# Moving the two buffers of split weights to the far end of SBUF

## The chip, the cores and the metric

The kernel runs on one core of one Trainium2 chip. The metric is the device time of one execution in microseconds (us), less is better.

## What the reference computes

A stack of transformer-like blocks in float32 on 512 positions of width 1024. Almost all its arithmetic is in dense projections, of which only the shapes matter here; what is computed between them is shown by name.

```python
# first block: norm, input projection 1024 -> 4096, two branches, output projection 2048 -> 1024
u = rms_norm(h, norm_in_g[l])
proj = jnp.einsum('bsd,de->bse', u, w_in[l])
pool_x, pool_z, m_x, m_z = jnp.split(proj, ...)
y_pool = pool_mixer(pool_x, ...) * jax.nn.silu(pool_z)
y_m = mlstm_branch(m_x, ...) * jax.nn.silu(m_z)
h = h + jnp.einsum('bse,ed->bsd', jnp.concatenate([y_pool, y_m], -1), w_out[l])
# second block, two layers: attention (nsa, then swa), then a feed-forward with a short convolution
x = x + mixer(rms_norm_2(x, norm_mix[i]), ...)
a, u = jnp.split(h @ w_gu, 2, axis=-1)          # 1024 -> 2 x 2816
x = x + (jax.nn.silu(causal_depthwise_conv(a, ...)) * u) @ w_down   # 2816 -> 1024
```

## The kernel before

All activations live in SBUF as eight channel tiles of 128 partitions x 512 positions. Every dense projection is made of **weight tiles**: one is 1024 x 128 weights, stored in SBUF as [128, 8, 128] float32 (4 KB in each partition). There are 227 of them, always in one fixed order, in these stages: "in" 32 tiles, "wo_pool" and "wo_m" 8 each, "nsa" 21, "nsa_o" 8, "gu0" 44, "down0" 22, "swa" 10, "swa_o" 8, "gu1" 44, "down1" 22.

To keep float32 accuracy at the rate of the `float32r` type, both operands are split into a high and a low part, and each product is made of three matmuls: high x high, high weights x low activations, low weights x high activations. So a weight tile costs 8 x 3 = 24 matmuls of 128 x 128 weights on 512 columns, 5448 in all. They are written at three places of the code with the same body: L1304 to L1306 (`channel_major`), L1602 to L1604 (the loop of the "gu" stages), L1616 to L1618 (the "down" stages).

Four engines work in a chain on the weight tiles, tied by semaphores alone:

- SyncE (SP) loads tile w into `raw`, which has 4 slots, by one transfer of 512 KB, once POOL has split tile w-4.
- GpSimd (POOL) waits until the matmuls of tile w-2 are done (`tile_used`), then makes the high part, L334: `WH[w % 2] = raw + 0`, and from it the low part, L337: `WL[w % 2] = raw - WH[w % 2]`. `WH` and `WL` have 2 slots each. They are the buffers that the change moves.
- TensorE (PE) waits for the split (`tile_split`) and for a free PSUM bank (`freed`) and does the 24 matmuls. Its weights come from `WH` and `WL`, its moving operand from `XH` and `XL`, the split activations.
- VectorE (DVE) and ScalarE (ACT) take the results out of PSUM, do all the elementwise work on buffers in `arena`, and write `XH` and `XL`.

Everything that isn't named by itself (intermediate tensors of each stage, of the attentions too) is carved out of one buffer, `arena`, of 30712 float32 per partition. Matmuls outside of the projections read both operands from it, as L1342 (32 records of 128 x 512, plain float32) does.

SBUF buffers are placed one behind the other in the order of their declaration. In KB from the first one, per partition:

| buffer | before | after |
|---|---|---|
| `resid` | 0 to 16 | same |
| `x_hi` (`XH`) | 16 to 32 | same |
| `x_lo` (`XL`) | 32 to 48 | same |
| `raw` | 48 to 64 | same |
| `w_hi` (`WH`) | 64 to 72 | 199.4 to 207.4 |
| `w_lo` (`WL`) | 72 to 80 | 191.4 to 199.4 |
| nine small ones (`cols`, `ident`, `masks`, `rstd`, ...) | 80 to 87.4 | 64 to 71.4 |
| `arena` | 87.4 to 207.4 | 71.4 to 191.4 |
| `zero`, `mv`, `rv`, `dn` | from 207.4 | same |

These lines declare them (`P` is 128, `KT` 8, `S` 512, `RAW` 4, `SPL` 2):

```python
R = sb("resid", [P, KT, S])
XH = sb("x_hi", [P, KT, S], F32R)
XL = sb("x_lo", [P, KT, S], F32R)
raw = sb("raw", [P, RAW, KT, P])
WH = sb("w_hi", [P, SPL, KT, P], F32R)
WL = sb("w_lo", [P, SPL, KT, P], F32R)
```

and these lines read the moved buffers, in `channel_major`:

```python
mm(out, WH[:, s, k], XH[:, k], start=(k == 0), stop=False)
mm(out, WH[:, s, k], XL[:, k], start=False, stop=False)
ins = mm(out, WL[:, s, k], XH[:, k], start=False, stop=(k == KT - 1))
```

Of the kernel before, what the change touches and what calls it, by code (L numbers as in the profile page):

```python
# [18 lines left out]
F32R = mybir.dt.float32r  # L19
# [5 lines left out]
P = 128  # L25
# [3 lines left out]
KT = D // P  # L29
# [22 lines left out]
SPL = 2  # L52
# [65 lines left out]
def build(nc, a):  # L118
    with ExitStack() as ctx:
        def sb(name, shape, dt=F32):  # L120
            return ctx.enter_context(nc.sbuf_tensor("sb_" + name, shape, dt))
# [6 lines left out]
        XH = sb("x_hi", [P, KT, S], F32R)  # L128
        XL = sb("x_lo", [P, KT, S], F32R)
        raw = sb("raw", [P, RAW, KT, P])  # L130
        WH = sb("w_hi", [P, SPL, KT, P], F32R)
        WL = sb("w_lo", [P, SPL, KT, P], F32R)
        cols = sb("cols", [P, NCOL])
        rows = sb("rows", [P, NROW])
        ident = sb("ident", [P, P])
# [6 lines left out]
        PS = ctx.enter_context(nc.psum_tensor("ps", [P, 8, S], F32))  # L142
        NA = 30712
        arena = sb("arena", [P, NA])

        def col(name, k=0):
            return cols[:, COLS[name] + k:COLS[name] + k + 1]
# [146 lines left out]
        def psum(bank, n=S):  # L294
            return PS[:, bank, 0:n]
# [32 lines left out]
        def _(pool):  # L328
            def split(it, s, first=False):

                pool.wait_ge(raw_in[s], 16 * (it + 1))
                if not first:
                    pool.wait_ge(tile_used, 4 * it + (s - SPL + 1))
                nc.gpsimd.tensor_tensor(WH[:, s % SPL], raw[:, s], zero.unsqueeze(2).broadcast_to([P, KT, P]), ALU.add  # L334
                                        ).then_inc(hi_made, 1)
                pool.wait_ge(hi_made, 4 * it + (s + 1))
                nc.gpsimd.tensor_tensor(WL[:, s % SPL], raw[:, s], WH[:, s % SPL].bitcast(F32),  # L337
                                        ALU.subtract).then_inc(tile_split, 1)
# [933 lines left out]
        def _(pe):  # L1272
# [19 lines left out]
            def channel_major(stage, j, n, xname=None):  # L1292
# [6 lines left out]
                for k in range(KT):  # L1299
# [3 lines left out]
                    out = psum(t % 2)  # L1303
# [3 lines that stand above are left out]
                ins.then_inc(tile_used, 1)  # L1307
# [280 lines left out]
            def ffn(layer, q):  # L1588
# [7 lines left out]
                with pe.Fori(1, FT // 2) as it:  # L1596
                    for b in range(4):
# [3 lines left out]
                        for k in range(KT):  # L1601
# [3 lines that stand above are left out]
                        ins.then_inc(tile_used, 1)  # L1605
                pe.wait_ge(freed, t0 + 2 * FT - 1)
                last = (t0 + 2 * FT - 1) % 2
                for f in range(FT):
# [4 lines left out]
                    for k in (sorted(range(KT), key=lambda k: k == last) if f == 0 else range(KT)):  # L1613
# [3 lines left out]
                        mm(psum(k), WH[:, s, k], XL[:, x], start=False, stop=False)  # L1617
                        ins = mm(psum(k), WL[:, s, k], XH[:, x], start=False, stop=(f == FT - 1))  # L1618
                        if f == FT - 1 and k < KT - 1:
# [151 lines left out]
```

## Time and profile before

| | |
|---|---|
| median of 2 runs | 1889.88 us (1889.49 to 1890.26) |
| span of the profiled execution | 1889.5 us |
| instructions | 22388 |
| PE busy | 1708.0 us, 90% of the span |
| DVE busy | 1169.6 us, 62% |
| POOL busy | 1058.6 us, 56% |
| mean granted TensorE clock | 0.961 |

The span reaches from the first to the last instruction; the timed executions stand within 0.8 us of it. Records of matmuls overlap, since the engine is pipelined: what tells its pace is the time from one start to the next, not the length of a record.

### The profile page before, as it was taken

To read this page: it belongs to the slowest core of one execution; us is meant where nothing else is said; L and a number is where in the kernel's file an instruction comes from. 1 tells how busy PE (TensorE), PEld (TensorE's weight loads), DVE (VectorE), ACT (ScalarE), POOL (GpSimd) and SP (SyncE) were. 2 spreads that over 40 slices of the span, in tenths; PEclk is the share of its full clock that TensorE was granted. 3 is DMA by queue.
4 is the path that set the end of the run, shared out by engine and by line. 5 is a ranking of instruction groups with operands and counts; after the bars stand their busy time and mean duration, and the time that the engine had idled before them with its cause. 6 is when DMAs were issued, how large, how long until landed. Compare 5 with 4: busy or idle time off the path is not lost.

```text
span 1889.5 us, 22388 instructions
## 1 busy us (share of the span) xinstructions
PE 1708.0 (90%) x8180; PEld 1346.3 (71%) x8180; DVE 1169.6 (62%) x1503; ACT 386.3 (20%) x719; POOL 1058.6 (56%) x472
## 2 busy tenths in 40 slices
PE   6688999898877979999899998998799899998996
PEld 4566845566666867778688887886678788887885
DVE  7995133557898347764676776336954576767334
ACT  3000123332200134442211111112143211111112
POOL 5566712137665310003688887886701688888784
PEclk8899999999988989999999999999989999999998
DMA  5122301014221100001233332332200223333231
GB/s 212 57 88 67 101 23 34 12 45 150 78 78 56 45 23 1 1 1 34 78 100 89 100 100 78 99 91 89 89 1 12 84 94 90 99 100 90 80 98 56
DMA packets 37545, 133.47 MB, mean 71 GB/s; under 512 B 4560, under 2 KB 4960, under 8 KB 36960
## 3 DMA queue, kind: packets, MB, share of 16 engines
q1 hardware_dynamic: 34992, 123.22, 21.3%
q10 hardware_dynamic: 2480, 9.22, 1.3%
q8 instruction: 52, 0.85, 0.2%
q14 instruction: 21, 0.17, 0.0%
HBM read 130.33 MB, written 2.10 MB: 70 GB/s over the span
## 4 chain that ended last, share of the span: by engine, by line
PE 75%; DVE 19%; issue 2%; ACT 2%; POOL 1%; DMA 0%; DVEq 0%; ACTq 0%; SPq 0%; POOLq 0%
PE ps L1602 8%; PE ps L1603 8%; PE ps L1604 8%; PE ps L1304 7%; PE ps L1305 7%; PE ps L1306 7%; PE ps L1563 5%; PE ps L1616 4%; PE ps L1618 4%; PE ps L1617 4%; PE ps L1531 3%; PE ps L1546 2%; DVE sb_arena L764 2%; DVE sb_arena L992 2%; PE ps L1331 2%
## 5 line engine op out<-in xcount | busy, mean ns | idle before, releaser
L334 POOL TENSOR_TENSOR sb_w_hi<-sb_raw,sb_zero 128x1024 fp32r<-128x1024 f32 x227 | 449.7, 1981 | 778.5 <-PE ps L1306 663.8
L337 POOL TENSOR_TENSOR sb_w_lo<-sb_raw,sb_w_hi 128x1024 fp32r<-128x1024 f32 x227 | 590.7, 2602 | 17.8
L1304 PE MATMUL ps<-sb_x_hi,sb_w_hi 128*128 128x512 f32 x824 | 340.8, 414 | 97.3 <-DVE sb_arena L971 24.6
L1305 PE MATMUL ps<-sb_x_lo,sb_w_hi 128*128 128x512 f32 x824 | 330.9, 402 | 0.0
L1306 PE MATMUL ps<-sb_x_hi,sb_w_lo 128*128 128x512 f32 x824 | 330.1, 401 | 0.0
L1304 PEld LDWEIGHTS ps<-sb_x_hi,sb_w_hi 128*128 128x128 f32 x824 | 161.6, 196 | 150.0 <-issue 28.9
L1602 PE MATMUL ps<-sb_x_hi,sb_w_hi 128*128 128x512 f32 x640 | 249.8, 390 | 0.0
L1604 PE MATMUL ps<-sb_x_hi,sb_w_lo 128*128 128x512 f32 x640 | 249.3, 389 | 0.0
L1603 PE MATMUL ps<-sb_x_lo,sb_w_hi 128*128 128x512 f32 x640 | 249.2, 389 | 0.0
L1306 PEld LDWEIGHTS ps<-sb_x_hi,sb_w_lo 128*128 128x128 f32 x824 | 160.8, 195 | 35.6
L1305 PEld LDWEIGHTS ps<-sb_x_lo,sb_w_hi 128*128 128x128 f32 x824 | 161.6, 196 | 33.7 <-issue 1.7
L1189 DVE TENSOR_TENSOR sb_x_lo<-sb_arena,sb_x_hi 128x512 fp32r<-128x512 f32 x44 | 77.2, 1765 | 134.5 <-ACT sb_x_hi L625 134.5
L1616 PE MATMUL ps<-sb_x_hi,sb_w_hi 128*128 128x512 f32 x352 | 139.0, 395 | 11.5 <-DVE sb_x_lo L1189 11.5
L1602 PEld LDWEIGHTS ps<-sb_x_hi,sb_w_hi 128*128 128x128 f32 x640 | 120.1, 188 | 29.6 <-POOL sb_w_lo L337 3.3
L1617 PE MATMUL ps<-sb_x_lo,sb_w_hi 128*128 128x512 f32 x352 | 138.6, 394 | 0.0
L1618 PE MATMUL ps<-sb_x_hi,sb_w_lo 128*128 128x512 f32 x352 | 138.4, 393 | 0.0
L1604 PEld LDWEIGHTS ps<-sb_x_hi,sb_w_lo 128*128 128x128 f32 x640 | 120.1, 188 | 25.4
L1603 PEld LDWEIGHTS ps<-sb_x_lo,sb_w_hi 128*128 128x128 f32 x640 | 120.2, 188 | 23.6
L1201 DVE SCALAR_TENSOR_TENSOR sb_arena<-sb_arena,sb_cols 128x512 f32<-128x512 f32 x44 | 112.4, 2554 | 6.7 <-DVE sb_arena L1199 6.7
L617 ACT ACTIVATE sb_arena<-sb_arena 128x512 f32<-128x512 f32 x44 | 27.8, 633 | 416.6 <-DVE sb_arena L1203 416.6
L1563 PE MATMUL ps<-sb_arena 128*128 128x96 f32 x864 | 105.4, 274 | 0.0
L1563 PEld LDWEIGHTS ps<-sb_arena 128*128 128x128 f32 x864 | 101.9, 193 | 0.0
(240 smaller groups left out, 2182.3 us busy)
## 6 DMA issues: line engine op xcount, KB each, us to landing
sb_raw<-in_w SPq DMA_DIRECT2D x227, 512.0 KB, 3.6
sb_resid<-in_x SPq DMA_DIRECT2D x8, 256.0 KB, 5.5
sb_arena<-in_cmp_w1k ACTq DMA_DIRECT2D x1, 2048.0 KB, 11.0
sb_arena<-in_cmp_w1v ACTq DMA_DIRECT2D x1, 2048.0 KB, 14.2
out<-sb_resid SPq DMA_DIRECT2D x8, 256.0 KB, 2.1
sb_arena<-in_pool_w ACTq DMA_DIRECT2D x1, 1024.0 KB, 5.0
sb_arena<-in_invc ACTq DMA_DIRECT2D x1, 1024.0 KB, 7.0
sb_arena<-in_wg ACTq DMA_DIRECT2D x1, 768.0 KB, 8.4
```

Source lines behind the costliest of these rows:

```text
L334: nc.gpsimd.tensor_tensor(WH[:, s % SPL], raw[:, s], zero.unsqueeze(2).broadcast_to([P, KT, P]), ALU.add).then_inc(hi_made, 1)
L337: nc.gpsimd.tensor_tensor(WL[:, s % SPL], raw[:, s], WH[:, s % SPL].bitcast(F32), ALU.subtract).then_inc(tile_split, 1)
L1304: mm(out, WH[:, s, k], XH[:, k], start=(k == 0), stop=False)
L1305: mm(out, WH[:, s, k], XL[:, k], start=False, stop=False)
L1306: ins = mm(out, WL[:, s, k], XH[:, k], start=False, stop=(k == KT - 1))
L1563: ins = mm(PS[:, v % 2, to:to + VN], PT_[:, v % 2, hh, p0:p0 + P], v_rows[0 if swa else m][:, at:at + VN], start=(n == 0), stop=(n == len( ...
L1602: mm(out, WH[:, s, k], XH[:, k], start=(k == 0), stop=False)
L1603: mm(out, WH[:, s, k], XL[:, k], start=False, stop=False)
L1604: ins = mm(out, WL[:, s, k], XH[:, k], start=False, stop=(k == KT - 1))
L1616: mm(psum(k), WH[:, s, k], XH[:, x], start=(f == 0), stop=False)
L1617: mm(psum(k), WH[:, s, k], XL[:, x], start=False, stop=False)
L1618: ins = mm(psum(k), WL[:, s, k], XH[:, x], start=False, stop=(f == FT - 1))
```

## The change

`WH` and `WL` are declared behind `arena` instead of behind `raw`, in the order `WL`, `WH`. Everything that stood between (the small buffers and `arena`) moves down by 16 KB. The sizes, the number of slots and every instruction of every engine, with its order and its waits, are the same; only SBUF addresses differ. All shifts of `WH`, `WL` and `arena` are multiples of 128 bytes.

```diff
         raw = sb("raw", [P, RAW, KT, P])
-        WH = sb("w_hi", [P, SPL, KT, P], F32R)
-        WL = sb("w_lo", [P, SPL, KT, P], F32R)
         cols = sb("cols", [P, NCOL])
         rows = sb("rows", [P, NROW])
...
         NA = 30712
         arena = sb("arena", [P, NA])
+        WL = sb("w_lo", [P, SPL, KT, P], F32R)
+        WH = sb("w_hi", [P, SPL, KT, P], F32R)
```

## Rows read from the trace of the kernel before

**Rows 1.** The page: busy time, and tenths busy in 40 slices

```profile
PE 1708.0 (90%) x8180; PEld 1346.3 (71%) x8180; DVE 1169.6 (62%) x1503; ACT 386.3 (20%) x719; POOL 1058.6 (56%) x472
...
PEclk8899999999988989999999999999989999999998
```

**Rows 2.** Busy time of each engine in the stages gu0, down0 and nsa_o

```profile
core 0: us, PE busy (x) PEld busy (x) DVE busy (x) ACT busy (x) POOL busy (x), PEclk, DMA share, GB/s
...
870.00:913.50 43.50, 43.50 (x195) 35.92 (x192) 16.95 (x17) 5.70 (x10) 31.66 (x14) 1.00 0.25 73
919.30:1163.80 244.50, 243.63 (x1058) 198.62 (x1058) 170.14 (x139) 29.63 (x36) 198.70 (x86) 0.99 0.31 92
1169.80:1290.90 121.10, 121.03 (x528) 100.08 (x528) 40.06 (x28) 11.18 (x18) 95.95 (x42) 0.99 0.32 96
```

**Rows 3.** Groups: line, engine, operation, count | busy us, mean ns | idle before

```profile
L337 POOL TENSOR_TENSOR sb_w_lo<-sb_raw,sb_w_hi 128x1024 fp32r<-128x1024 f32 x227 | 590.7, 2602 | 17.8
L334 POOL TENSOR_TENSOR sb_w_hi<-sb_raw,sb_zero 128x1024 fp32r<-128x1024 f32 x227 | 449.7, 1981 | 778.5 <-PE ps L1306 663.8 <-PE ps L1604 59.5 <-PE ps L1618 48.4
L1304 PE MATMUL ps<-sb_x_hi,sb_w_hi 128*128 128x512 f32 x824 | 340.8, 414 | 97.3 <-DVE sb_arena L971 24.6 <-DVE sb_x_lo L683 23.7 <-DVE sb_arena L779 14.9
L1602 PE MATMUL ps<-sb_x_hi,sb_w_hi 128*128 128x512 f32 x640 | 249.8, 390 | 0.0
L1616 PE MATMUL ps<-sb_x_hi,sb_w_hi 128*128 128x512 f32 x352 | 139.0, 395 | 11.5 <-DVE sb_x_lo L1189 11.5
```

**Rows 4.** PE in gu0: first matmuls of two tiles, 24 apart

```profile
1011.10 0.39 PE L1602 MATMUL ps<-sb_x_hi,sb_w_hi 128*128 128x512 f32 x1
...
1016.54 0.40 PE L1602 MATMUL ps<-sb_x_hi,sb_w_hi 128*128 128x512 f32 x1
```

**Rows 5.** PE in nsa_o while POOL is idle, three matmuls apart, and POOL's next instruction

```profile
872.83 0.39 PE L1304 MATMUL ps<-sb_x_hi,sb_w_hi 128*128 128x512 f32 x1
...
873.51 0.39 PE L1304 MATMUL ps<-sb_x_hi,sb_w_hi 128*128 128x512 f32 x1
...
875.86 1.90 POOL L334 TENSOR_TENSOR sb_w_hi<-sb_raw,sb_zero 128x1024 fp32r<-128x1024 f32 x1 [194.94 <-PE ps L1306]
```

**Rows 6.** PE in order of time: arena operands at full clock; projections at half clock

```profile
12.80 0.63 PE L1304 MATMUL ps<-sb_x_hi,sb_w_hi 128*128 128x512 f32 x1
13.23 0.63 PE L1305 MATMUL ps<-sb_x_lo,sb_w_hi 128*128 128x512 f32 x1
...
238.81 13.90 PE L1342 MATMUL ps<-sb_arena 128*128 128x512 f32 x32
```

**Rows 7.** Line L1342 by itself: duration of one record, ns, least, median, most

```profile
L1342 PE MATMUL ps<-sb_arena x32: 590/592/595, 238.8 to 252.1; 128*128 128x512 f32 x32
```

**Rows 8.** POOL over two tiles of gu0, and the weight load that waits for it

```profile
1005.94 1.90 POOL L334 TENSOR_TENSOR sb_w_hi<-sb_raw,sb_zero 128x1024 fp32r<-128x1024 f32 x1 [0.50 <-PE ps L1604]
1007.92 2.46 POOL L337 TENSOR_TENSOR sb_w_lo<-sb_raw,sb_w_hi 128x1024 fp32r<-128x1024 f32 x1
1011.41 2.17 POOL L334 TENSOR_TENSOR sb_w_hi<-sb_raw,sb_zero 128x1024 fp32r<-128x1024 f32 x1 [1.04 <-PE ps L1604]
1013.66 2.72 POOL L337 TENSOR_TENSOR sb_w_lo<-sb_raw,sb_w_hi 128x1024 fp32r<-128x1024 f32 x1
1016.43 0.19 PEld L1602 LDWEIGHTS ps<-sb_x_hi,sb_w_hi 128*128 128x128 f32 x1 [0.16 <-POOL sb_w_lo L337]
```

**Rows 9.** Line L337 by itself: durations, and who waited for it

```profile
L337 POOL TENSOR_TENSOR sb_w_lo<-sb_raw,sb_w_hi x227: 2339/2717/3247, 7.1 to 1861.1; 128x1024 fp32r<-128x1024 f32 x114
...
  PEld ps L1602: 3.3, 19
```

**Rows 10.** Line L358, POOL on two inputs in the arena

```profile
L358 POOL TENSOR_TENSOR sb_arena<-sb_arena x8: 1265/1722/1735, 428.6 to 441.4; 128x512 f32<-128x512 f32 x8
```

**Rows 11.** POOL in down0, one tile

```profile
1253.28 1.90 POOL L334 TENSOR_TENSOR sb_w_hi<-sb_raw,sb_zero 128x1024 fp32r<-128x1024 f32 x1 [0.81 <-PE ps L1618]
1255.26 2.72 POOL L337 TENSOR_TENSOR sb_w_lo<-sb_raw,sb_w_hi 128x1024 fp32r<-128x1024 f32 x1
```

## Prediction, made before the change was run

> **What bounds the kernel now.** I read the page first. TensorE is busy for 90% of the span, and its granted clock is at nine tenths or more in nearly all slices [rows 1]. So the question is what sets the pace of PE, and where it waits. The view of the stages answers both: in gu0, down0 and nsa_o PE is busy for all but 1 us or less of the whole stretch [rows 2]. These stages, with gu1, down1 and swa_o, which have the same code, are 148 of the 227 weight tiles (44 + 22 + 44 + 22 + 8 + 8), and there the end moves only if a tile of 24 matmuls takes another time, or if PE has to wait for its weights.
>
> The pace: the same matmul of two neighbouring tiles of gu0 starts at 1011.10 and at 1016.54, 24 matmuls apart, which is 5.44 us or **226.7 ns** for each [rows 4]. There are 3 x (824 + 640 + 352) = 5448 such matmuls [rows 3], and 5448 x 226.7 ns = 1235 us, 65% of the span. This is the number that a placement of buffers could touch with the greatest effect.
>
> The weights: POOL makes them just in time. In gu0 it sits idle for 0.50 us before one tile and 1.04 us before the next, always until PE frees the slot; the split of the second takes 2.17 + 2.72 us against 1.90 + 2.46, since DVE works in the arena beside it; and at its end PE's weight load waits for it, by 0.16 us [rows 8]. Over the run these waits of L1602 come to 3.3 us in 19 places [rows 9]. So one tile in two of the gu stages has about 0.03 us of slack (0.50 less the handover of some 0.47 that the waiting tile leaves), the other about 0.54; in down0 POOL idles 0.81 us [rows 11], a slack of 0.31.
>
> **The change part by part.** No instruction is added, removed or moved on any engine, so there is no term for issue, for waits or for DMAs. Three things have another address: the targets of POOL's L334 and L337, the weights that PE loads for the 5448 matmuls, and everything in the arena, 16 KB lower. Each is costed by asking whether the trace shows any time that depends on where an operand lies, or on two engines being in the same region.
>
> 1. *PE reading weights while others write beside them.* If POOL's writes into `WH` and `WL`, or transfers into `raw` next to them, disturbed PE, its pace would differ when POOL is idle. POOL is idle for 194.94 us before its L334 at 875.86; in that time the matmuls of L1304 at 872.83 and 873.51 are three apart, 0.68 us, or 226.7 ns each, as in gu0 under a busy POOL [rows 5, 4]. POOL's traffic costs PE nothing, so moving it away gives nothing: 0 us.
>
> 2. *PE's two own reads, weights and moving operand, colliding.* The tile of rows 4 covers eight k slices of `WH`, of `WL`, of `XH` and of `XL`, at distances from some 16 to some 64 KB from each other, and its neighbour the other slot. If 226.7 ns depended on those distances, single starts would differ. They do not: 23 intervals of a tile that starts without a wait are 0.22 or 0.23 us. The pace in nsa_o is that of gu0 though both slots are used there. I take 0 us. What speaks for a gain is that 226.7 is not the best the engine shows. At half clock the same matmuls start 0.43 us apart, that is 512 columns at 1.2 GHz and nothing on top [rows 6], so 213.3 would be the counterpart at 2.4 GHz. And the 32 records of L1342, whose operands both lie in the arena, span 13.90 us with a last record of 0.59, so 13.31 / 31 = 429.4 ns for twice the work of a split matmul, 214.7 for its share [rows 6, 7]. The difference of 12.0 ns on each of 5448 is 65 us at most; but L1342 is plain float32 at half the column rate, so the type explains the difference at least as well as the place. The bounds are 0 and -65 us, and I take the end 0, since it goes by rows of the same instruction.
>
> The Trainium skill, page TensorE: Matmul & The Clock Gate, section "Wait — 56ns, not 53.3ns?", gives a spacing of N / 2.4 GHz plus about 2.5 ns, 215.7 ns for 512 columns, for a stream at full clock. This trace disagrees for split matmuls, with 226.7 [rows 4]. By the page's figure each would have 11 ns to lose, an estimate of 60 us for all; the same page gives weight loads and moving operands read ports of their own (section "Step-by-step: what each phase is for"), which leaves no collision that a move could undo.
>
> 3. *POOL's two passes.* They write to a new place. POOL's other elementwise work shows what another place costs: L358 works on 512 elements with both inputs and the output in the arena, 30 KB and more from `WH`, and takes 1265 ns at the least; L337 takes 2339 at the least for 1024 [rows 10, 9]. The second 512 elements cost 1074 ns, 2.1 ns an element, and leave 191 ns for the start of an instruction, so one rate with one start-up fits both places. So 0 us. As a bound I allow 5% either way of the 4.58 us of a split (2602 + 1981 ns, rows 3), 0.23 us, because eight records of L358 can't show less. Dearer, it would cost 0.23 - 0.03 = 0.20 us on 44 tiles of the gu stages, 8.8 us, and nothing where the slack is 0.31 or more. Cheaper, it would save the waits of 3.3 us, and I allow 1.7 us for slower first matmuls behind them: -5 us.
>
> 4. *Arena and small buffers 16 KB lower.* DVE, ACT and PE read and write them at hundreds of different offsets already, and the shift is a multiple of 128 bytes, so no pattern inside a line changes. 0 us; bound included in that of point 3, since DVE matters to the end mainly through POOL.
>
> The sum is 0: the profiled execution would again have a span of 1889.5 us, and the median, which was 0.4 us above that, 1889.9. The forecast is **1889.9 us**, with bounds of its own of -5 and +8.8, so 1885 to 1898.7.
>
> **The rivals.** *Faster: weights and activations stop colliding.* The one state in which PE does 512 columns in less time is L1342, and the move makes the distance between `WH`/`WL` and `XH`/`XL` large, some 150 KB and more instead of 16 to 64. If the 12 ns per matmul were a matter of sharing a region, a tile would take 24 x 214.7 = 5.15 us, 0.29 less. But not all of that is granted: in the gu stages every second tile is then limited by POOL and gains 0.03 only, so 44 x 0.29 + 44 x 0.03 = 14.1 us; down0 and down1, 44 x 0.29 = 12.8 (slack 0.31); nsa_o, swa_o, wo_pool and wo_m, 32 x 0.29 = 9.3; in, nsa and swa, 63 tiles, where PE waits for DVE often (L1304 has 97.3 us of idle time before it [rows 3]), between 0 and 18.3, say 9. Sum 45 us: **1845 us** (1836 to 1854). Against it: the pace is uniform over all distances in a tile, and the excess is gone at half clock. Chance 0.09.
>
> *Slower: POOL becomes the bound.* If POOL writes or reads back more slowly near the end of SBUF, every split grows by some d. It decides from d = 0.03 us on, in every second tile of gu0 and gu1, where PE already waits for L337 [rows 8, 9]. The price is 44 x (d - 0.03) + 60 x (d - 0.31), the second term for down0, down1, nsa_o and swa_o. 2% or 37.8 us is reached at d = 0.56 us, a split dearer by 12%. With 15%, 0.69 us, it is 29 + 23 + 44 x 0.15 for the other gu tiles = 58 us: **1948 us**. For it speaks only that POOL has so little slack; against it the one rate of point 3. Chance 0.04.
>
> *It isn't a change at all.* That buffers are declared in another order and land where they did is excluded by the sizes, which put `w_lo` at 191.4 KB. That the move matters to nothing is the forecast itself.
>
> **How the numbers follow.** Forecast 0.87, faster rival 0.09, slower rival 0.04. The range needs 8 in 10; the forecast's own case with its bounds gives that, so it stays with 1884 to 1898 (its +8.8 rounded down, its -5 widened by 1 us for clock windows that fall otherwise; 2 of the executions shown differ by 0.8). A change of 2%, 37.8 us, is about what a measurement of this kernel can tell from none. The faster rival's 1836 to 1854 lies on both sides of 1852, mostly under it, so faster by over 2% gets 0.07. Slower by over 2% gets 0.03, as a POOL dearer by 5 to 12% stays within it. Within 2%: 0.90.
>
> **What would show it in the profile after.** Starts of L1602, L1304 and L1616 still 0.22 or 0.23 us apart (5.44 us a tile): points 1 and 2 hold. Starts 0.215 apart: the faster rival. L334 at 1.90 us without DVE beside it and L337 at 2.34 to 2.72, POOL idle 0.5 and 1.0 us in turn in gu0: point 3 holds. L337 beyond 2.9, and waits of PE's weight loads for L337 well over 3.3 us in total: the slower rival. DVE's groups within 1% of before: point 4. The prediction is wrong if an engine's time depends on the region of SBUF in a way that this layout, with `WH` and `WL` always between `raw` and the small buffers, gave no chance to see; the uniform pace only speaks for distances under 64 KB.

## The result and the profile after

The changed kernel takes 1916.12 us (1915.7 to 1916.55, 2 runs) against 1889.88: ratio 1.0138, 95% interval [1.0119, 1.0157]. That is 26.2 us slower, outside the forecast range of 1884 to 1898. The profiled execution has a span of 1913.9 us, 24.4 more than before, at the same mean granted clock, 0.961.

First the groups of the kernel after, as [rows 3] (count | busy us, mean ns | idle before):

```profile
L337 POOL TENSOR_TENSOR sb_w_lo<-sb_raw,sb_w_hi 128x1024 fp32r<-128x1024 f32 x227 | 592.8, 2611 | 17.8
L334 POOL TENSOR_TENSOR sb_w_hi<-sb_raw,sb_zero 128x1024 fp32r<-128x1024 f32 x227 | 445.4, 1962 | 804.8 <-PE ps L1306 671.1 <-PE ps L1604 73.1 <-PE ps L1618 53.7
L1304 PE MATMUL ps<-sb_x_hi,sb_w_hi 128*128 128x512 f32 x824 | 344.4, 418 | 91.9 <-DVE sb_x_lo L683 30.2 <-DVE sb_arena L971 24.0 <-DVE sb_arena L779 11.7
...
L1602 PE MATMUL ps<-sb_x_hi,sb_w_hi 128*128 128x512 f32 x640 | 252.7, 395 | 0.0
```

POOL, the engine of the slower rival, is not slower: L337 went from 2602 to 2611 ns in the mean, L334 from 1981 to 1962, and POOL waits longer for PE than before (804.8 us against 778.5). It is the matmuls that take longer. The line of L1602 by itself, as the source view shows it, has no wait for POOL left, where [rows 9] had 3.3 us in 19 places:

```profile
L1602 PEld LDWEIGHTS ps<-sb_x_hi,sb_w_hi x640: 187/188/192, 946.9 to 1762.2; 128*128 128x128 f32 x160
L1602 PE MATMUL ps<-sb_x_hi,sb_w_hi x640: 390/393/404, 947.1 to 1762.5; 128*128 128x512 f32 x160
its engine sat idle before it (us, times) until:
who waited for it (us, times):
```

The pace is read from starts, as in [rows 4]. PE in gu1 after, first matmuls of two tiles, 24 apart, and a piece of the stream from the first of them:

```profile
1572.75 0.40 PE L1602 MATMUL ps<-sb_x_hi,sb_w_hi 128*128 128x512 f32 x1
1572.98 0.39 PE L1603 MATMUL ps<-sb_x_lo,sb_w_hi 128*128 128x512 f32 x1
1573.21 0.40 PE L1604 MATMUL ps<-sb_x_hi,sb_w_lo 128*128 128x512 f32 x1
1573.45 0.39 PE L1602 MATMUL ps<-sb_x_hi,sb_w_hi 128*128 128x512 f32 x1
...
1578.35 0.40 PE L1602 MATMUL ps<-sb_x_hi,sb_w_hi 128*128 128x512 f32 x1
```

A tile takes 5.60 us here, 233.3 ns a matmul, where it took 5.44 and 226.7. The nanoseconds of the trace show the difference more plainly than two decimals. Before, the starts of an undisturbed tile are 227, 226, 227, 227, 226, 227 ns apart and so on, and in the stages at full clock a tile that began late falls back into that within eleven matmuls at most. After, they never settle on one interval: in gu1 they alternate 238, 229, 238, 229 (mean 233.3), and in gu0 and the down stages they repeat 230, 233, 241, 232, 231, 232, 228, seven in a round with a mean of 232.4. The round of seven drifts through tiles of 24, so it belongs neither to a k slice nor to a slot. POOL has no part in it: it rests for 194.7 us before its L334 at 876.84, and in that time the 23 matmuls of nsa_o from 871.19 to 876.53 take 5.34 us, 232.2 ns each, where the kernel before had 226.7 [rows 5].

At half clock nothing changed, and neither did L1342, plain float32 from the arena. The second tells little: both of its operands lie in the arena, so the change left their distance as it was. After, PE at 11.44 us, and line L1342 by itself, to be held against [rows 6, 7]:

```profile
11.44 0.63 PE L1304 MATMUL ps<-sb_x_hi,sb_w_hi 128*128 128x512 f32 x1
11.86 0.63 PE L1305 MATMUL ps<-sb_x_lo,sb_w_hi 128*128 128x512 f32 x1
```

```profile
L1342 PE MATMUL ps<-sb_arena x32: 590/592/592, 237.4 to 250.7; 128*128 128x512 f32 x32
```

Where the 24.4 us lie is seen in the windows from the first to the last matmul of each stage. After, for nsa_o, gu0 and down0, then swa, gu1 and down1 (columns as in [rows 2]):

```profile
870.80:915.40 44.60, 44.60 (x195) 36.14 (x193) 17.04 (x17) 5.79 (x10) 31.72 (x14) 1.00 0.23 71
921.10:1170.10 249.00, 248.06 (x1058) 200.15 (x1058) 170.46 (x139) 29.77 (x36) 197.04 (x86) 0.99 0.29 91
1176.00:1300.60 124.60, 124.55 (x528) 100.81 (x528) 40.18 (x28) 11.17 (x18) 96.18 (x42) 0.98 0.30 93
1303.40:1374.10 70.70, 62.12 (x242) 47.86 (x242) 64.30 (x61) 15.22 (x24) 44.83 (x19) 0.91 0.22 68
...
1512.40:1763.00 250.60, 250.00 (x1058) 200.35 (x1058) 168.91 (x139) 29.71 (x36) 197.69 (x86) 0.99 0.29 90
1768.80:1893.90 125.10, 124.96 (x528) 101.21 (x529) 40.28 (x28) 14.62 (x24) 91.83 (x40) 0.98 0.23 72
```

The same windows of the kernel before, for swa, gu1 and down1:

```profile
1293.80:1360.40 66.60, 59.77 (x242) 46.84 (x242) 62.26 (x60) 15.15 (x24) 44.81 (x19) 0.95 0.25 72
...
1497.40:1741.00 243.60, 242.75 (x1058) 198.26 (x1058) 168.51 (x139) 29.71 (x36) 199.24 (x86) 0.99 0.31 93
1747.00:1869.60 122.60, 122.53 (x528) 101.23 (x529) 40.19 (x28) 14.68 (x24) 91.64 (x40) 0.98 0.24 73
```

Against these and [rows 2], gu0 grew by 4.5 us (244.5 to 249.0), down0 by 3.5, nsa_o by 1.1, swa by 4.1, gu1 by 7.0, down1 by 2.5. The same windows give 2.4 for nsa (186.5 to 188.9), 1.2 for swa_o (43.5 to 44.7), 0 for the two "wo" stages together and -1.4 for "in". Full price would be 24 x 5.8 ns = 0.14 us for a tile at a pace of 232.5, or 6.1 us for 44 tiles, and 0.16 us or 7.0 us at the 233.3 of gu1. From the start of the fifth tile to that of the last the two stages pay less, 4.7 us instead of 5.4 in gu0 and 5.5 instead of 6.2 in gu1: their former waits for POOL and the slow first matmuls behind them went away.

Most of the rest is clock. In the first 6 us of gu1 the granted clock was 0.74 before and 0.52 after, and the first tile took 1.3 us more; in gu0 it was 0.63 and 0.74, and the first tile took 0.6 us less. Part of what swa lost is clock too: 0.95 before, 0.91 after. In "in" the last tiles, which follow one another without a wait, did grow by 0.16 us each; the stage as a whole, where PE waits for DVE and for transfers and the stretches of half clock fell otherwise, did not.

### The profile page after: what moved, and what is told of

Same layout as the page of the kernel before. It is cut to its first block, busy times and chain, and to the rows that moved or that the text cites. A ratio compares the mean times of both kernels' runs of the same rounds, so it can differ in the third digit from the quotient of the medians.

```text
span 1913.9 us, 22388 instructions
## 1 busy us (share of the span) xinstructions
PE 1737.9 (91%) x8180; PEld 1354.7 (71%) x8180; DVE 1171.4 (61%) x1503; ACT 386.2 (20%) x719; POOL 1056.4 (55%) x472
## 4 chain that ended last, share of the span: by engine, by line
PE 75%; DVE 19%; issue 2%; ACT 2%; POOL 1%; DMA 0%; DVEq 0%; ACTq 0%; SPq 0%; POOLq 0%
PE ps L1603 8%; PE ps L1602 8%; PE ps L1604 8%; PE ps L1304 7%; PE ps L1305 7%; PE ps L1306 7%; PE ps L1563 5%; PE ps L1616 4%; PE ps L1617 4%; PE ps L1618 4%; PE ps L1531 3%; PE ps L1546 2%; DVE sb_arena L764 2%; DVE sb_arena L992 2%; PE ps L1331 1%
## 5 line engine op out<-in xcount | busy, mean ns | idle before, releaser
L334 POOL TENSOR_TENSOR sb_w_hi<-sb_raw,sb_zero 128x1024 fp32r<-128x1024 f32 x227 | 445.4, 1962 | 804.8 <-PE ps L1306 671.1
L337 POOL TENSOR_TENSOR sb_w_lo<-sb_raw,sb_w_hi 128x1024 fp32r<-128x1024 f32 x227 | 592.8, 2611 | 17.8
L1304 PE MATMUL ps<-sb_x_hi,sb_w_hi 128*128 128x512 f32 x824 | 344.4, 418 | 91.9 <-DVE sb_x_lo L683 30.2
L1305 PE MATMUL ps<-sb_x_lo,sb_w_hi 128*128 128x512 f32 x824 | 335.9, 408 | 0.0
L1306 PE MATMUL ps<-sb_x_hi,sb_w_lo 128*128 128x512 f32 x824 | 335.6, 407 | 0.0
L1604 PE MATMUL ps<-sb_x_hi,sb_w_lo 128*128 128x512 f32 x640 | 252.7, 395 | 0.0
L1602 PE MATMUL ps<-sb_x_hi,sb_w_hi 128*128 128x512 f32 x640 | 252.7, 395 | 0.0
L1603 PE MATMUL ps<-sb_x_lo,sb_w_hi 128*128 128x512 f32 x640 | 252.6, 395 | 0.0
L1616 PE MATMUL ps<-sb_x_hi,sb_w_hi 128*128 128x512 f32 x352 | 140.9, 400 | 11.3 <-DVE sb_x_lo L1189 11.3
L1602 PEld LDWEIGHTS ps<-sb_x_hi,sb_w_hi 128*128 128x128 f32 x640 | 120.3, 188 | 28.8
L1604 PEld LDWEIGHTS ps<-sb_x_hi,sb_w_lo 128*128 128x128 f32 x640 | 120.3, 188 | 28.6
L1617 PE MATMUL ps<-sb_x_lo,sb_w_hi 128*128 128x512 f32 x352 | 140.5, 399 | 0.0
L1618 PE MATMUL ps<-sb_x_hi,sb_w_lo 128*128 128x512 f32 x352 | 140.4, 399 | 0.0
L1201 DVE SCALAR_TENSOR_TENSOR sb_arena<-sb_arena,sb_cols 128x512 f32<-128x512 f32 x44 | 112.7, 2560 | 6.7 <-DVE sb_arena L1199 6.7
```

The lines of the kernel that those rows point to most:

```text
L1616: mm(psum(k), WH[:, s, k], XH[:, x], start=(f == 0), stop=False)
```

## The experiments

All addresses that matter are put in one number here, the **phase**: the address of a weight buffer less that of the activations, modulo 256 bytes. Within `WH`, `WL`, `XH`, `XL` a k slice is 512 or 2048 bytes and a slot 4096, so all slices of a buffer have one phase. The kernel before has phase 0, since its buffers of 16 and 8 KB follow each other without a gap. The changed one has 128: the small buffers and the arena that now lie ahead add up to 384 bytes more than a multiple of 512, and 384 is 128 more than 256.

The first theory, formed on the trace above: the pace depends on the phase, not on how far the buffers are apart. The rival: it depends on the region, since the weights lie far from the activations or near the end of SBUF. A third: the shift of the arena did it. A fourth is left open by the first runs: the weights moved by 128 bytes against `raw` too, from which POOL makes them, and not only against the activations.

### Far away, old phase

`WH`, `WL` behind arena and `ident`; the arena is 120 words shorter, which no stage uses; the rest of the small buffers last.

```diff
+NA = 30592
 R = sb("resid", [P, KT, S])
...
 raw = sb("raw", [P, RAW, KT, P])
+arena = sb("arena", [P, NA])
+ident = sb("ident", [P, P])
 WH = sb("w_hi", [P, SPL, KT, P], F32R)
 WL = sb("w_lo", [P, SPL, KT, P], F32R)
```

> The two buffers lie behind the arena (120 KB and more above the activations) as in the changed kernel, but at addresses that are the old ones modulo 4096 bytes, so modulo 512 the weights and the activations stand to each other as before. Theory of the phase (the pace of split matmuls depends on where weights and moving operand lie to each other within some 512 bytes): 226.7 ns from start to start as before, time within 0.3% of 1889.9 us. Rival, the region (far from the activations, or high in SBUF, weights are read more slowly): 232 to 233 ns, 1914 to 1918 us.

Measured: 1890.08 us (10 runs), ratio 1.0 [0.999, 1.001]. The pace is 226.7 ns in every stage; first matmuls of two neighbouring tiles of down0:

```profile
1209.61 0.39 PE L1616 MATMUL ps<-sb_x_hi,sb_w_hi 128*128 128x512 f32 x1
...
1215.05 0.39 PE L1616 MATMUL ps<-sb_x_hi,sb_w_hi 128*128 128x512 f32 x1
```

5.44 us, as before. The region rival is dead, and so is an effect of the arena's shift, which here is 23.4 KB instead of 16.

### Near, new phase

Four small buffers (taken from their old places) lie between `raw` and the weights.

```diff
 raw = sb("raw", [P, RAW, KT, P])
-WH = sb("w_hi", [P, SPL, KT, P], F32R)
-WL = sb("w_lo", [P, SPL, KT, P], F32R)
+rstd = sb("rstd", [P, S])
+cmask = sb("cmask", [P, NT, P], BF16)
+rows = sb("rows", [P, NROW])
+mv = sb("mv", [P, 16, 2])
+WL = sb("w_lo", [P, SPL, KT, P], F32R)
+WH = sb("w_hi", [P, SPL, KT, P], F32R)
```

> The two buffers stay next to the activations, 3.4 KB above their old place, at addresses that are those of the changed kernel modulo 4096 (rstd, cmask, rows and mv lie between raw and them; the arena hardly moves). Theory of the phase: the slow pace, 232 to 233 ns a matmul, 1912 to 1920 us. Rival, the region: 226.7 ns, 1890 us. A third theory, that the arena's shift by 16 KB did it: 226.7 ns, 1890 us as well.

Measured: 1916.04 us (4 runs), ratio 1.0144 [1.0127, 1.0161], the whole loss of the change with the two buffers 3.4 KB above their old place. Tiles of down0:

```profile
1218.80 0.40 PE L1616 MATMUL ps<-sb_x_hi,sb_w_hi 128*128 128x512 f32 x1
...
1224.37 0.39 PE L1616 MATMUL ps<-sb_x_hi,sb_w_hi 128*128 128x512 f32 x1
```

5.57 us a tile, 232.1 ns, and the same round of seven intervals in the trace as in the changed kernel.

### Everything 128 bytes up

```diff
+sb("gap0", [P, 32])
 R = sb("resid", [P, KT, S])
```

> Every buffer lies 128 bytes higher, in the old order, so all distances stay and all absolute addresses modulo 512 change. If only the distance between weights and moving operand counts: 226.7 ns, 1890 us. If the absolute address of the weights modulo 256 or 512 counts (before 128, in the changed kernel 0, here 256): another pace than 226.7, about that of the changed kernel or worse, over 1905 us. The region rival expects 1890 us.

Measured: 1890.18 us (10 runs), ratio 1.0001 [0.9992, 1.0011], pace 226.7 ns. The distance counts, not the address.

### Two phases in one kernel

The two slots become buffers of their own; slot 0 gets phase 128, slot 1 256, which is 0 again.

```diff
+sb("gap0", [P, 32])
+WH0 = sb("w_hi0", [P, KT, P], F32R)
+WL0 = sb("w_lo0", [P, KT, P], F32R)
+sb("gap1", [P, 32])
+WH1 = sb("w_hi1", [P, KT, P], F32R)
+WL1 = sb("w_lo1", [P, KT, P], F32R)
```

> Slot 0 of both weight buffers lies 128 bytes further from the activations than before (modulo 512), slot 1 256 bytes further; both near. Tiles alternate between the slots, so the trace shows a pace for each. Theory of the phase: at least one of the two slots shows another pace than 226.7 ns, as the changed kernel does at 384 bytes; if the period is 256 bytes, slot 1 shows 226.7 and slot 0 what the changed kernel shows, 232 to 233. The region rival: 226.7 in both.

Measured: 1905.18 us in one run, somewhat over half of the loss. Tiles alternate. First matmuls of three tiles of down0 (L1631 is L1616 of the kernel before):

```profile
1213.67 0.40 PE L1631 MATMUL ps<-sb_x_hi,sb_w_hi 128*128 128x512 f32 x1
...
1219.26 0.39 PE L1631 MATMUL ps<-sb_x_hi,sb_w_hi 128*128 128x512 f32 x1
...
1224.71 0.40 PE L1631 MATMUL ps<-sb_x_hi,sb_w_hi 128*128 128x512 f32 x1
```

Slot 0 takes 5.59 us, slot 1 5.45. So the period is 256 bytes: with a divisor of it, slot 0 would be fast too. It also takes the last doubt from the run before: slot 0 of `WH` lies at the very address that `WH` had there, and is slow here, since the activations are 128 bytes lower.

### The other phases

The same two-slot form with other gaps: 64 and 128 bytes for the first run, 32 and 64 for the second, 160 (slot 1 first) and 64 for the third; for the fourth the high and low part of a slot are one buffer that is read from its fifth word on.

> Both weight slots near; slot 0 stands 64 bytes, slot 1 192 bytes further from the activations than before. 0 and 256 gave 226.7 ns, 128 and 384 gave 232.5. If what counts is one address bit of weight 128 (two halves of 128 bytes each in a period of 256), the value at 64 should be that of 0 or of 128, and one of 64 and 192 like 226.7 and the other like 232.5, or both between. If the pace grows evenly with the distance from a multiple of 256, both slots show about 229.6. A pace under 226.7 at 64 or 192 would make a faster kernel than both, by some 5 us for each ns.

> As the run at 64 and 192, with slot 0 at 32 bytes and slot 1 at 96 bytes. An address bit of weight 128 that is compared at the start of the buffers would leave 226.7 in both; an even growth gives about 228.2 and 231.1; with finer structure, anything else. No figure is forecast beyond the span from 215 to 240 ns.

> Near, slot 0 at 224 and slot 1 at 160 bytes modulo 256. With 0 at 226.7 ns, 32 at 233.5, 64 at 233.3, 96 at 234.5, 128 at 232.5 and 192 at 228.7, a smooth course would give 227 to 229 at 224 and 229 to 232 at 160. A value under 226.7 would show that the old place isn't the best; else 0 stays the only good one.

> Near, slot 0 at 16 and slot 1 at 240 bytes modulo 256 (high and low part of a slot in one buffer). If the chip works on lines of 32 bytes, 16 is as 0 or as 32 (226.7 or 233.5), and 240 as 224; if the course is smooth, 240 is within 1 ns of 226.7. It tells how exact the placement has to be.

Measured: 1915.47, 1915.44, 1920.09 and 1912.21 us, one run each. The pace by phase is the median over the tiles of gu0 at full clock, from a tile's eleventh matmul on, out of the starts in the traces. It takes in only 13 intervals of a tile, so a round that does not fit into them moves it: over whole tiles phase 16 has 233.0, phase 96 has 234.0, phase 160 has 233.0.

| phase, bytes | ns a matmul in gu0 | elsewhere |
|---|---|---|
| 0 | 226.7 | same |
| 16 | 233.4 | 226.7 in down0 |
| 32 | 233.5 | same |
| 64 | 233.5 | 233.2 in down0 |
| 96 | 234.5 | same |
| 128 | 232.5 | 233.3 (whole tiles) in gu1 of the changed kernel |
| 160 | 233.6 | same |
| 192 | 228.8 and 233.4, tile by tile | the same two in gu1, 228.7 in down0 |
| 224 | 233.3 | same |
| 240 | 228.4 | 226.6 in down0 |

None of my guesses of a form held: no single address bit, no even growth, no smooth course. Phase 0 is the only one that has 226.7 throughout; most others give 232 to 234.5, and 16 and 240 fall back to 226.7 in one stage. None is below 226.7 but for rounding.

Phase 192 has two paces in one stage. Its tiles in slot 1 alternate between them in gu0 and in gu1, though PE reads the same addresses in each. First matmuls of one such tile and the next tile, then of the following one in slot 1 (L1617 is L1602 of the kernel before):

```profile
994.07 0.40 PE L1617 MATMUL ps<-sb_x_hi,sb_w_hi 128*128 128x512 f32 x1
...
999.58 0.40 PE L1617 MATMUL ps<-sb_x_hi,sb_w_hi 128*128 128x512 f32 x1
...
1005.17 0.40 PE L1617 MATMUL ps<-sb_x_hi,sb_w_hi 128*128 128x512 f32 x1
...
1010.78 0.39 PE L1617 MATMUL ps<-sb_x_hi,sb_w_hi 128*128 128x512 f32 x1
```

The one takes 5.51 us, the other 5.61. So at this phase the pace depends on something beside PE's addresses, the state in which the stream comes into a tile, say; no run shows what. With two phases in one kernel, the value of one slot may also owe something to its neighbour.

### Which operand

First the parts of the weights apart: slot 0 has `WH` at 128 and `WL` at 0, slot 1 the reverse.

```diff
+WH1 = sb("w_hi1", [P, KT, P], F32R)
+WL0 = sb("w_lo0", [P, KT, P], F32R)
+sb("gap0", [P, 32])
+WH0 = sb("w_hi0", [P, KT, P], F32R)
+WL1 = sb("w_lo1", [P, KT, P], F32R)
```

> Slot 0 has its high part at 128 bytes and its low part at 0, slot 1 the high part at 0 and the low part at 128. If each of the 24 matmuls is slowed by the weight load that runs beside it, at 128 alone, the slot with two of three loads at 128 (slot 0) gets about 230.6 ns in the mean and the other about 228.6; if one pair alone is responsible, one slot shows 226.7 and the other 232.5.

Measured: 1917.38 us in one run; slot 0 233.2 ns, slot 1 231.2. Slot 1, with its low part alone at 128, repeats three intervals in the trace: 226 from the high-high matmul to the next, then 234 and 233 or 234. A piece of gu0 (L1616 to L1618 are L1602 to L1604 of the kernel before):

```profile
1016.09 0.39 PE L1616 MATMUL ps<-sb_x_hi,sb_w_hi 128*128 128x512 f32 x1
1016.31 0.40 PE L1617 MATMUL ps<-sb_x_lo,sb_w_hi 128*128 128x512 f32 x1
1016.54 0.40 PE L1618 MATMUL ps<-sb_x_hi,sb_w_lo 128*128 128x512 f32 x1
1016.78 0.39 PE L1616 MATMUL ps<-sb_x_hi,sb_w_hi 128*128 128x512 f32 x1
```

The load of the low weights starts in the trace with the matmul that streams `XL`, at 1016.32. That matmul's step to the next is slow (234 ns), and so is the step after it; the record of the load itself stays at 0.19 us. So one bad load in three costs more than a third, 4.5 ns of the 5.8, and two in three (slot 0) cost more than all three: 6.5 ns. The means of 228.6 and 230.6 that I expected for single prices that add up are refuted.

Then the activations: `XL` goes 128 bytes up, `raw` and the weights 256, so the weights have phase 0 to `XH` and to `raw` and 128 to `XL` alone.

```diff
 XH = sb("x_hi", [P, KT, S], F32R)
+sb("gap0", [P, 32])
 XL = sb("x_lo", [P, KT, S], F32R)
+sb("gap1", [P, 32])
 raw = sb("raw", [P, RAW, KT, P])
```

> The weights stay at 0 to the high activations, and the low activations are moved by 128 bytes against both, so one matmul in three streams an operand that stands at 128 to the weights. If only the distance between the weights being loaded and the operand being streamed counts: a mean between 226.7 and 232.5, some 228.6 ns. If the distance of weights to high activations alone counts: 226.7.

Measured: 1913.85 us in one run; 230.8 ns in gu0 and nsa_o, 233.3 in gu1 and both down stages. The weights kept their phase to `XH`, so the streamed operand is the partner in it. They kept it to `raw` too, which answers the fourth rival: what this run has in common with all slow ones is that weights and `XL` stand to each other at another phase than 0. The size was again above the proportional guess.

### The change with its phase mended

```diff
-        NA = 30712
+        NA = 30616
         arena = sb("arena", [P, NA])
         WL = sb("w_lo", [P, SPL, KT, P], F32R)
         WH = sb("w_hi", [P, SPL, KT, P], F32R)
```

> The changed kernel with an arena that is 96 words (384 bytes) shorter, words that no stage uses: the two buffers lie at 191 KB as in the change, and at a multiple of 256 bytes from the activations. If the distance modulo 256 is all that made the change slower: 226.7 ns a matmul and 1889 to 1891 us. If something else of this layout costs too (the order of the two buffers, the arena's place), it stays above 1895 us.

Measured: 1890.91 us (11 runs), ratio to the kernel before 1.0002 [0.9993, 1.0011]. 384 bytes less of unused arena take back the whole loss. Its groups read as those of before:

```profile
L337 POOL TENSOR_TENSOR sb_w_lo<-sb_raw,sb_w_hi 128x1024 fp32r<-128x1024 f32 x227 | 590.0, 2599 | 17.8
L334 POOL TENSOR_TENSOR sb_w_hi<-sb_raw,sb_zero 128x1024 fp32r<-128x1024 f32 x227 | 449.3, 1979 | 779.2 <-PE ps L1306 664.1 <-PE ps L1604 59.3 <-PE ps L1618 48.5
L1304 PE MATMUL ps<-sb_x_hi,sb_w_hi 128*128 128x512 f32 x824 | 341.8, 415 | 94.6 <-DVE sb_arena L971 24.6 <-DVE sb_x_lo L683 24.1 <-DVE sb_arena L759 14.4
```

No version beats the kernel before; with phase 0 the place is free to choose.

## Why the prediction was wrong, point by point

The reading of the bound was right: PE's pace is what sets the end, and the loss is a matter of that pace alone. I had named it as the number that a placement could touch with the greatest effect, and then costed it at 0.

**Point 2 failed**, "PE's two own reads, weights and moving operand, colliding", taken at the end 0 with bounds of 0 and -65 us. The whole loss belongs to it, +26.2 us in the time and +24.4 in the span: the run with the phase mended takes it back. It is 5448 matmuls at up to 5.8 or 6.6 ns each, less what waits and clock gave back. The argument was that a tile covers many distances, from 16 to 64 KB, and shows one pace. But all those distances are multiples of 512 bytes, so the two tiles sample one phase 48 times. It could speak for the region, where it was right (the run far away shows 0 us), and not for the low bits of the address. My closing caveat went the same wrong way: it doubted distances beyond 64 KB, not the phase. The bound had the wrong side as well: I asked what would be gained if a collision stopped, not what would be lost if the old layout was the good one of its kind. The exact pace of 226.7 [rows 4, 5] is what one phase gives as well as what no dependence gives; I took it as proof of the second.

**Point 4** rested on the same slip: "a multiple of 128 bytes, so no pattern inside a line changes". The period is 256 bytes, and the weights moved by 128 against it. For the arena itself the point held: DVE's L1201 took 2554 ns before and 2560 after, and L1342 kept its 592 ns.

**Point 1** held: far from or near to POOL's and the transfers' targets, the pace is that of the phase. **Point 3** held: L334 and L337 kept their durations within 1% at a place 119 and 135 KB further up, and the slower rival's mechanism did not occur (POOL's idle time grew).

**The faster rival** had the right pair of operands and the wrong variable and sign. Its 12 ns over L1342 are not phase: no phase among ten came below 226.7. The slower side had a chance of 0.04 for POOL alone; a slower PE was not among the cases. That the time stayed within 2%, to which the prediction gave 0.90, came true for another reason than the one given.

The Trainium skill, page SBUF — State Buffer, section "Who interferes with whom", says that PE and ACT never wait on anyone, and the page TensorE: Matmul & The Clock Gate, section "Step-by-step: what each phase is for", gives weight loads and moving operand read ports of their own. By the two together the ten phases would be equal. The measurements decide against that for split matmuls at full clock: 226.7 ns at phase 0 and up to 234.5 ns at others, with no change but in addresses.

What stays open is the circuit behind it. That the weights and the streamed operand are the two partners is shown for `WL` and `XL`, by the runs on high or low parts and on `XL`; for the other pairs it is taken over from them. That two reads of SBUF collide in time is only argued: from the intervals that never settle at a bad phase, and from the same 427 ns at half clock in both kernels.

Plain float32 was hardly tried. By the declarations both operands of L1342 have phase 0 to each other, before and after. The eight records of L1639, whose weights are `ones` and whose moving operand lies in the arena, stand by the declarations at phase 112 in the kernel before and 16 in the run far away; from the second on they start 428 to 430 ns apart in both, as L1342 does. That speaks for no effect, on few records. Why 226.7 and not 214.7 is the best pace is open too, and so is why gu0 and gu1, with the same addresses, fall into rounds of 232.4 and 233.3.

## What to carry to other kernels

When a kernel streams float32r matmuls of this shape (128 x 128 weights, a load for each, 512 columns) back to back at full clock, place the weight buffers at a multiple of 256 bytes from the moving operand, slices and slots included, and write that down beside the declarations; other shapes and types were not tried: a small buffer or an odd arena size declared ahead of them costs 1.4% here without changing one instruction. Whether a weight buffer is near or far didn't matter. And to argue from "all these cases show the same", list first in which variable the cases differ at all; here they differed in kilobytes and agreed in the low bits.

## What the hardware showed that was not expected

- The pace of split matmuls depends on the distance of weights and moving operand modulo 256 bytes: 226.7 ns at 0, and 228.4 to 234.5 in gu0 at nine other values, the nearest of them 16 bytes away.
- The effect is not a price for each load that adds up: one load in three at phase 128 brings the mean to 231.2, two to 233.2, all at 128 to 232.5, and some phases show two paces in one execution (226.7 and 233.4 at 16 bytes; 228.8 and 233.4 in alternating tiles with the same addresses at 192).
- It is absent at half clock, 0.42 to 0.43 us from start to start before and after.
